# Two fp32r products of specially rounded factors in place of three, in every split projection

## The reference

```python
proj = h @ w_in[i]                       # first block: q, k, v, z_a, b, c, u, z_c, each 512 wide
mixed = jnp.concatenate([attn, conv_out], axis=-1) @ w_out[i]
x = x + jax.nn.sigmoid(x @ w_ple_gate[i]) * e
...
parts = jnp.split(n @ w_in[l], offsets, axis=-1)   # second block: c_q, c_kv, k_pe, gq, gk, gv, ga, gg, gates
y_a = mla_branch(...)                              # 8 heads, 512 + 16 tokens
y_b = gla_branch(...)                              # 4 heads, gated linear attention
mix = sigmoid(gate_a) * (y_a @ w_o_mla) + sigmoid(gate_b) * (y_b @ w_o_gla)
h = h + mix @ w_out
# 8 heads of queries, the 16 best of 128 x 128 experts for each token and head, then gelu(h u) v
h = h + peer_ffn(rmsnorm(h, norm_ffn), peer_w_q, peer_keys, peer_u, peer_v)
```

## Time and profile before

| | us |
|---|---|
| runs | 2175.26, 2175.35 (median), 2179.72 |
| span of the profiled execution | 2175.9 |
| TensorE busy | 2115.4 |
| VectorE busy | 1304.1 |
| ScalarE busy | 922.6 |
| GpSimd busy | 1033.5 |

### The profile page before, as it was taken

How to read it: one execution, slowest core, us unless ns; L and a number is a source line. 1 busy time by engine, 2 the same in 40 slices (tenths; PEclk the granted TensorE clock), 3 DMA queues, 4 the chain that set the end, 5 groups by cost and what they waited for, 6 DMA issues and landing times.

```text
span 2175.9 us, 27394 instructions
## 1 busy us (share of the span) xinstructions
PE 2115.4 (97%) x10296; PEld 1661.6 (76%) x10296; DVE 1304.1 (60%) x2244; ACT 922.6 (42%) x1528; POOL 1033.5 (47%) x892
## 2 busy tenths in 40 slices
PE   8999999999999999999999998999999899999999
PEld 6877767557887776887878877777778788888887
DVE  6456257352235774215898957888881666666664
ACT  4223343572234234111334447777773434343432
POOL 6655546212324122877859887999996100000000
PEclk9999999999999999999999999999999999999999
DMA  5222312201111111233216664777788988888884
GB/s 201 100 78 78 116 61 90 90 30 49 59 40 59 59 55 43 97 122 110 78 59 199 205 206 141 272 289 246 272 291 294 333 300 286 289 284 300 288 287 149
DMA packets 98291, 359.32 MB, mean 165 GB/s; under 512 B 8480, under 2 KB 41504, under 8 KB 73328
## 3 DMA queue, kind: packets, MB, share of 16 engines
q1 hardware_dynamic: 98160, 357.56, 47.3%
HBM read 286.09 MB, written 71.30 MB: 164 GB/s over the span
## 4 chain that ended last, share of the span: by engine, by line
PE 67%; POOL 13%; DVE 11%; issue 6%; ACT 2%; DMA 1%; POOLq 0%; SPq 0%; ACTq 0%; DVEq 0%
PE ps L1438 11%; PE ps L1439 11%; PE ps L802 10%; PE ps L803 9%; PE ps L804 9%; POOL area L2643 6%; POOL wring_parts L2621 6%; PE ps L791 2%; PE ps L1249 2%; DVE area L2413 2%; PE ps L1386 1%; PE ps L1387 1%; DVE area L2410 1%; PE ps L884 1%; PE ps L1225 1%
## 5 line engine op out<-in xcount | busy, mean ns | idle before, releaser
L2577 POOL CAST wring_parts<-wring 128x512 fp32r<-128x512 f32 x236 | 170.5, 764 | 546.0 <-PE ps L804 429.3
L1386 PE MATMUL ps<-sqbuf_parts,wring_parts 128*128 128x512 f32 x1024 | 412.6, 403 | 5.5 <-POOL wring_parts L2621 5.5
L1387 PE MATMUL ps<-normed_x_parts,wring_parts 128*128 128x512 f32 x1024 | 404.4, 395 | 0.0
L2621 POOL TENSOR_TENSOR wring_parts<-wring_parts,wring 128x512 fp32r<-128x512 f32 x256 | 331.0, 1323 | 76.0 <-ACT wring_parts L1856 73.0
L2581 POOL TENSOR_TENSOR wring_parts<-wring,wring_parts 128x512 fp32r<-128x512 f32 x244 | 351.2, 1470 | 6.6 <-ACT wring_parts L1852 1.5
L1386 PEld LDWEIGHTS ps<-sqbuf_parts,wring_parts 128*128 128x128 f32 x1024 | 194.0, 189 | 50.6 <-POOL wring_parts L2621 4.9
L1387 PEld LDWEIGHTS ps<-normed_x_parts,wring_parts 128*128 128x128 f32 x1024 | 193.9, 189 | 41.8
L802 PE MATMUL ps<-resid_parts,wring_parts 128*128 128x512 f32 (+1 forms) x528 | 201.2, 381 | 6.1 <-DVE normed_x_parts L2010 3.3
L803 PE MATMUL ps<-normed_x_parts,wring_parts 128*128 128x512 f32 (+1 forms) x528 | 197.0, 373 | 0.0
L804 PE MATMUL ps<-resid_parts,wring_parts 128*128 128x512 f32 (+1 forms) x528 | 196.2, 372 | 0.0
L1474 ACT ACTIVATE area<-ps 128x1024 f32<-128x1024 f32 (+6 forms) x89 | 61.7, 696 | 275.2 <-PE ps L804 183.5
(11 more groups left out here) (269 smaller groups left out, 4431.4 us busy)
## 6 DMA issues: line engine op xcount, KB each, us to landing
wring<-in_weights_dram SPq DMA_DIRECT2D x65, 1024.0 KB, 4.8
wring<-in_uT_dram SPq DMA_DIRECT2D x128, 512.0 KB, 4.4
area<-in_vT_dram SPq DMA_DIRECT2D x44, 1024.0 KB, 7.2
hidden_table<-area SPq DMA_DIRECT2D x32, 1024.0 KB, 6.7
gate_table<-area SPq DMA_DIRECT2D x32, 1024.0 KB, 8.4
area<-gate_table SPq DMA_DIRECT2D x32, 1024.0 KB, 9.1
wring<-in_vT_dram SPq DMA_DIRECT2D x20, 1024.0 KB, 6.7
rt<-hidden_table SPq DMA_DIRECT2D x32, 512.0 KB, 4.6
```

The source lines that it names most:

```text
L1386: pe.matmul(out, first[:, d], h_first[:, k, :], start=(k == 0), stop=False)
L1387: mm = pe.matmul(out, rest[:, d], h_rest[:, k, :], start=False, stop=(k == KD - 1))
L2577: ins = nc.gpsimd.tensor_copy(up[:, d, :], W(name)[:, d, :])
L2621: ins = nc.gpsimd.tensor_tensor(rest[:, a:a + PIECE], first[:, a:a + PIECE], u_raw[t % len(USLOT)][:, a:a + PIECE], ALU.subtract)
```

## The change

- `three` becomes `two`: first by first, rest by rest. TensorE has 16 x 2 = 32 matmuls in a job of 256 columns, 1192 fewer in all.
- The factors change so that two products do: of activations, first = value/128 rounded, rest = 127 x first - value; of weights, first = value x 127/128 rounded, rest = first - value.
- ScalarE's roundings keep their number and get a scale. VectorE's subtractions (`tensor_tensor`) become `scalar_tensor_tensor`, of the same inputs. GpSimd's cast becomes `tensor_scalar` with a multiplication, its subtraction has its inputs swapped.
- All evictions multiply by 128: on ScalarE in the activation's scale, on VectorE by `scalar_tensor_tensor` in place of `tensor_tensor`.
- `Q_PARTS` is now `(h_first, h_rest)`. L1841 on ScalarE and L2435 on VectorE are gone, with their waits.

```diff
-        Q_PARTS = (blocks(16384), blocks(20480))
+        Q_PARTS = (h_first, h_rest)
...
-            def three(out, a_parts, b_parts, first, last):
-
-                (a_up, a_low), (b_up, b_low) = a_parts, b_parts
-                pe.matmul(out, a_up, b_up, start=first, stop=False)
-                pe.matmul(out, a_up, b_low, start=False, stop=False)
-                return pe.matmul(out, a_low, b_up, start=False, stop=last)
+            def two(out, a_parts, b_parts, first, last):
+
+                (a_first, a_rest), (b_first, b_rest) = a_parts, b_parts
+                pe.matmul(out, a_first, b_first, start=first, stop=False)
+                return pe.matmul(out, a_rest, b_rest, start=False, stop=last)
...
-            pe.wait_ge(h_split, 1)
...
-                    act.activation(h_upper[:, k, 0:width], normed_x[:, k, 0:width], ACT.Copy).then_inc(h_rounded_k, 1)
+                    act.activation(h_upper[:, k, 0:width], normed_x[:, k, 0:width], ACT.Copy,
+                                   scale=1.0 / SCALE).then_inc(h_rounded_k, 1)
...
-                copy_out(("k", m), kT[:, 2 * m:2 * m + 2, :], pair(("k", m)))
+                copy_out(("k", m), kT[:, 2 * m:2 * m + 2, :], pair(("k", m)), scale=float(SCALE))
...
-            act.activation(h_first, hs, ACT.Copy, scale=1.0 / SCALE).then_inc(h_rounded, 1)
...
-                dve.tensor_tensor(parts[1][:, k:k + 2, :], src[:, k:k + 2, :], parts[0][:, k:k + 2, :],
-                                  ALU.subtract).then_inc(pair_split, 1)
+                dve.scalar_tensor_tensor(parts[1][:, k:k + 2, :], parts[0][:, k:k + 2, :], float(SCALE - 1),
+                                         src[:, k:k + 2, :], ALU.mult, ALU.subtract).then_inc(pair_split, 1)
...
-                if h == 0:
-
-                    dve.wait_ge(h_rounded, 1)
-                    dve.scalar_tensor_tensor(h_rest, h_first, float(SCALE - 1), hs, ALU.mult, ALU.subtract
-                                             ).then_inc(h_split, 1)
-                else:
+                if h:
                     sum_places(h - 1)
...
-                        ins = nc.gpsimd.tensor_copy(up[:, d, :], W(name)[:, d, :])
+                        ins = nc.gpsimd.tensor_scalar(up[:, d, :], W(name)[:, d, :], GAIN, None, ALU.mult)
                     ins.then_inc(part_rounded, 1)
                     pool.wait_ge(part_rounded, i + 1)
                 for d in parts:
-                    ins = nc.gpsimd.tensor_tensor(low[:, d, :], W(name)[:, d, :], up[:, d, :], ALU.subtract)
+                    ins = nc.gpsimd.tensor_tensor(low[:, d, :], up[:, d, :], W(name)[:, d, :], ALU.subtract)
```

More of the change, by code:

```diff
@@ L824, in project_h @@
                             c = (m - tiles[0]) * 512 + at + (MF.start if width == TM else 0)
-                            mm = three(out[:, c:c + n], (up[:, k, d], low[:, k, d]),
+                            mm = two(out[:, c:c + n], (up[:, k, d], low[:, k, d]),
                                        h_parts(k, at, n), k == 0, k == KD - 1)
@@ L838, in project_parts @@
                             pe.wait_ge(pair_split, 4 * turn + n // 2 + 1)
-                        mm = three(pair(key)[:, m, :], (up[:, k, d], low[:, k, d]),
+                        mm = two(pair(key)[:, m, :], (up[:, k, d], low[:, k, d]),
                                    (parts[0][:, k, :], parts[1][:, k, :]), n == 0, n == KD - 1)
@@ L850, in tokens_h @@
                     for k in range(KD):
-                        mm = three(flat(key)[0:n, a * 256:a * 256 + 256], h_parts(k, t * P, n),
+                        mm = two(flat(key)[0:n, a * 256:a * 256 + 256], h_parts(k, t * P, n),
                                    (up[:, k, :], low[:, k, :]), k == 0, k == KD - 1)
@@ L925, in first_query @@
                         d = slice(a * P, (a + 1) * P)
-                        mm = three(pair(key)[:, a, :], (up[:, k, d], low[:, k, d]),
+                        mm = two(pair(key)[:, a, :], (up[:, k, d], low[:, k, d]),
                                    (FIRST_PARTS[0][:, k, :], FIRST_PARTS[1][:, k, :]), k == 0, k == KD - 1)
@@ L950, in first_value @@
                     for k in range(KD):
-                        mm = three(flat(key)[:, t * 256:t * 256 + 256],
+                        mm = two(flat(key)[:, t * 256:t * 256 + 256],
                                    (FIRST_PARTS[0][:, k, d], FIRST_PARTS[1][:, k, d]), (up[:, k, :], low[:, k, :]),
@@ L1236, in gate_quarter @@
                 for k in range(4 * (q % 2), 4 * (q % 2) + 4):
-                    mm = three(pair(key)[:, m, :], (up[:, k, d], low[:, k, d]), h_parts(k, 0, T), k == 0, k == KD - 1)
+                    mm = two(pair(key)[:, m, :], (up[:, k, d], low[:, k, d]), h_parts(k, 0, T), k == 0, k == KD - 1)
                 if q == 3:
@@ L1494, in root, with square_two @@
                 act.activation(r, r, ACT.Exp, scale=-0.5).then_inc(rooted, 1)
-            def square_two(name, m, src, width=T):
+            def square_two(name, m, src, width=T, scale=1.0):
                 k = NORM[name]
@@ L1521, in _ @@
             act.wait_ge(w_in[1], 16)
-            act.activation(W_parts("k0")[0], W("k0"), ACT.Copy).then_inc(part_rounded, 1)
+            act.activation(W_parts("k0")[0], W("k0"), ACT.Copy, scale=GAIN).then_inc(part_rounded, 1)
             act.wait_ge(first_consts, 32)
@@ L1564, in round_pair @@
                 act.wait_ge(pair_made, n + 1)
-                act.activation(parts[0][:, k:k + 2, :], src[:, k:k + 2, :], ACT.Copy).then_inc(pair_rounded, 1)
+                act.activation(parts[0][:, k:k + 2, :], src[:, k:k + 2, :], ACT.Copy,
+                               scale=1.0 / SCALE).then_inc(pair_rounded, 1)
             def copy_a(h):
@@ L1588, in _ @@
                     if g == "q":
-                        copy_out((g, m), qT[:, 2 * m:2 * m + 2, :], pair((g, m)))
+                        copy_out((g, m), qT[:, 2 * m:2 * m + 2, :], pair((g, m)), scale=float(SCALE))
                     if g == "k":
@@ L1641, in copy_tm @@
                 when_filled(act, key)
-                act.activation(dst[rows, 0:META], flat(key)[rows, MF.start + T:MF.stop], ACT.Copy)
-                empties(act.activation(dst[rows, META:TM], flat(key)[rows, MF.start:MF.start + T], ACT.Copy), key)
+                act.activation(dst[rows, 0:META], flat(key)[rows, MF.start + T:MF.stop], ACT.Copy, scale=float(SCALE))
+                empties(act.activation(dst[rows, META:TM], flat(key)[rows, MF.start:MF.start + T], ACT.Copy,
+                                       scale=float(SCALE)), key)
             copy_tm(("ckv", 0), ckv[:, 0, :])
@@ L1650, in _ @@
             when_filled(act, ("kpe", 0))
-            act.activation(gaT[0:16, :], flat(("kpe", 0))[0:16, MF], ACT.Copy)
+            act.activation(gaT[0:16, :], flat(("kpe", 0))[0:16, MF], ACT.Copy, scale=float(SCALE))
             copy_tm(("kpe", 0), kp, LATE)
@@ L1847, in query @@
                 if h >= 2:
-                    copy_out(("pq", h), pq[h % 2], pair(("pq", h)))
+                    copy_out(("pq", h), pq[h % 2], pair(("pq", h)), scale=float(SCALE))
                 if HP - 4 <= h < HP - 2:
```

75 lines of the change are left out of this document (38 added, 37 removed).

## The result

The changed kernel takes 2098.95 us (2097.94 to 2099.61), the kernel before 2177.06 us in the same comparison: a ratio of 0.9635 (0.9616 to 0.9653), 78 us less. The prediction had 2010 us with a range from 1978 to 2075. It is faster, as forecast, by less than half of the 167 us.

What follows compares the result with a forecast made beforehand. TensorE was taken to bound the kernel, with GpSimd setting the pace afterwards where jobs stand back to back. Stage savings summed to 167 us: 2175.9 - 167 = 2009, put at 2010 us, range 1978 to 2075.

Steps and rivals of the forecast that it cites:

- first attention: Attention of the first block: 44.9 us of matmuls go, 43 us saved, GpSimd having room among the attention units.
- the second: Second attention: 30.5 us of matmuls go, 29 us saved, as attention units stand between the jobs.
- `gg` to `w2`: Stage of 256 wide matmuls: 59.7 us go, only 37 saved, since GpSimd takes over the pace at 8.9 us.
- gated linear attention: Gated linear attention stage: 18.7 us of matmuls go, 15.7 us saved, head 0 losing some 3 to VectorE.
- the price of GpSimd's multiplication: GpSimd's weight splits: multiplication by a constant taken at the cast's price, 0.57 us each, two-input operation as upper bound.
- rival (a): GpSimd's multiplication costs as much as a two-input operation, 2.75 us more per group, 71 us in all: 2080 us; chance 0.13.
- the paced places: 24 groups in start, `wo`, `pg`, stage `gg` to `w2` and `pq`, where dearer multiplications would cost 66 us.
- `pg` to `kpe`: Stage `pg`, `cq`, `ckv`, `kpe`: 26.3 us of matmuls go, 12.9 saved, with hardly anything from `pg`.
- The queries: `pq0` to `pq7`: 10 us saved, from sooner scores 1.6, head 0's dropped operation 4.8, `pq7`'s shorter job 3.7.
- a falling clock: Sign of error: long TensorE idle time between jobs could lower its granted clock, 1.00 before; no size given.
- The transfers: Rival that weight transfers become the bound: DMA share still under 0.6, perhaps a few us at the start; no chance given.
- The rule for the price: The skill's 1.03 cycles per element: GpSimd multiplication of 512 columns 0.44 us, time some 12 to 15 us less.

Runs made afterwards that it cites:

- e1_cast: The changed kernel with GpSimd's old cast put back for the first parts of weights, factor 127/128 missing there: 2027.58 us, ratio 0.9292.
- e13_act_start: The changed kernel with ScalarE making most weights' first parts, q1 and k1 included, and six expert tiles split before head 2's weighing: 2010.62 us, ratio 0.9232.

## Why the prediction was wrong

- **The bound: right.** TensorE set the pace before, GpSimd after. In `e1_cast`, with groups of about the size that I had assumed, the terms for the first attention (42.8 for 43), the second (29.1 for 29), `gg` to `w2` (35.5 for 37) and gated linear attention (16.8 for 15.7) hold.
- **The step that failed: the price of GpSimd's multiplication.** "I take the cast's, since the inputs agree". Undisturbed, a multiplication of 128x512 measured 1.49 us against 0.61 for a cast, and four of them 5.85 against 2.29, which is 3.56 us more a group. It is over the two-input operation too, which I had as the upper bound (1.26 to 1.30). With the cast put back alone, 71 of the 89 us between 2010 and 2099 are gone. The number of inputs does not order these prices: one input costs 0.61 or 1.49, by the form.
- **The rival (a) had the mechanism, and its sum came near by luck.** Its 71 us for the multiplication are the 71 measured, but made up otherwise. In the paced places it had 66 and the stages lost 50 (`gg` to `w2` 36, start 4.5, `wo` 5.6, `pg` to `kpe` 0.3, queries 4.0). Among the attention units it had 5 and they lost 24 (18 and 6): with 10.9 to 11.1 us a group the first stage has no spare and is paced throughout. Two errors, the price of a group (2.75 for 3.56) and what the places make of it, cancelled. That (a) said 2080 and not 2099 comes from the 2009 below it, where `e1_cast` has 2028. The range ended at 2075, under (a)'s own sum: it took the nearest row above as the end of an unknown price.
- **`pg` to `kpe`: over-sized.** 12.9 was forecast; 6.3 came even with the cast. `pg`, of which I had hardly expected anything, gave 5.8 us (`ple` with it), though groups there took up to 13.0 us in `e1_cast`, not the 11.1 of the earlier trace rows:

```profile
275.28 5.46 POOL L2573 CAST wring_parts<-wring 128x512 fp32r<-128x512 f32 x4
280.81 7.45 POOL L2577 TENSOR_TENSOR wring_parts<-wring_parts,wring 128x512 fp32r<-128x512 f32 x4
```

  `cq` to `kpe` gave 0.4, and 1.1 in `e13_act_start`. TensorE waits there for VectorE's lower parts of `n` and for splits, and its granted clock is 0.82 over the stage, 0.96 before. Matmuls of 264 columns stand 0.22 us apart after the wait, where they stand 0.12 at full clock, as in the earlier trace rows:

```profile
312.42 0.59 PE L800 MATMUL ps<-resid_parts,wring_parts 128*128 128x264 f32 x1 [2.88 <-DVE normed_x_parts L2008]
...
318.12 0.42 PE L801 MATMUL ps<-normed_x_parts,wring_parts 128*128 128x264 f32 x1
318.34 0.42 PE L800 MATMUL ps<-resid_parts,wring_parts 128*128 128x264 f32 x1
```

  Its 72 third products were worth 11.4 us by my prices. Idle time grew by 6.6 us, and busy time fell by 7.0 only, which leaves some 4 for the lower clock. That is an estimate; no run isolates the clock. The prediction had named a falling clock as a sign and given it no price.
- **The queries: wrong.** "1.6 + 4.8 + 3.7 = 10" summed gains on head 0 and on `pq7`'s job; -5.1 came, -1.1 with the cast. The search began 26.6 us after `pq0`, not sooner than the 26.1 of before (1056.21 in the earlier trace rows); head 1 did begin 3.8 us nearer to head 0's start. But the stretch ends with head 7, and that came at 247 us with or without the operation, at 252 in the changed kernel. The terms held the places of the waits rightly (`pq7` still waits, 7.7 us in the changed kernel and 13.0 in `e1_cast`). They missed what lies behind: six more heads and the 44 tiles, in which TensorE had next to no idle time before and waits more for GpSimd now. That 10.9 us came in `e13_act_start` does not make the working right, since head 7 stood at 244 there.
- **What cost nothing, did.** VectorE's new forms and ScalarE's scales do not show: stages without GpSimd's splits are as before within 3.3 us. The transfers did not become the bound: DMA has 1% of the chain in the page above.
- **The rule for the price fell.** By the 1.03 cycles per element of the Trainium skill, "GPSIMD Engine Reference", section "3.1 Elementwise — side-by-side cycle accounting", a multiplication was estimated at 0.44 us, cheaper than mine. The trace has 1.49, 3.4 times that.

## What to carry to other kernels

When a change takes work from the engine that sets the pace, the next engine's cost per unit is the result. Take the price of a new instruction form on it from a row of that very form; where none is there, the neighbours (copy, two-input operation) are not bounds, and the range should reach to the point at which the gain is gone. For a chain between two engines, read its period and its last member; an operation removed from the first member may be worth nothing. Where a change gives TensorE idle time, look in the trace for stages in which its granted clock then falls.

## What the runs showed of the hardware

- On GpSimd a multiplication by a constant costs 0.21 us + 2.50 ns a column (128 to 1024 columns, 128 partitions, float32 in). At 512 columns it is the same whether it writes float32 or fp32r, and an addition of a constant costs the same. Row by row at 512 columns: the cast 0.61 us, the subtraction of two tensors 1.27, the multiplication 1.49.
- These prices hold while VectorE does nothing: 79 multiplications of the changed kernel without VectorE's work beside them took 1482 to 1497 ns, 71 casts of `e1_cast` 607 to 622. With it beside them for most of their time they took 1684 and 929 ns on average, and single ones up to 2719 and 1646.
- ScalarE does the same scaling and rounding of 128x1024 in about 1.05 us, as part of an activation. GpSimd's subtractions took 1.53 us on average beside it from `gg` to `w2`.
- TensorE's granted clock was 0.88 over the 182 us in which it was busy for 140, and 0.94 to 0.95 over the same stage in `e1_cast` and `e13_act_start`, where it was busy for nearly 90% of the time. At the lower of its two levels (1.2 in place of 2.4 GHz) matmuls of 512 columns stood 0.43 us apart in place of 0.23, after waits of 5.3 and of 3.1 and 3.7 us.
